# A two-layer hybrid decoder step on eight cores: first tiles on two rings, parameters and tiles for the second layer fetched earlier, squares in a buffer of their own

## The reference, cut to what matters

```
h = RMSNorm(x)
p = h @ w_in                      # 1024 -> 3456 columns
a_val, a_gate, a_z | b_h, b_b, b_c, b_z | c_u, c_v, c_z = split(p)
a   = a_val * sigmoid(a_gate)
y_a = silu(LayerNorm(conv31(a) + bias)) * silu(a_z)
y_b = b_b * conv3(b_c * b_h) * silu(b_z)
y_c = c_u * chunk_mix(LayerNorm(c_v)) * silu(c_z)   # causal 128x128 mix per head
x   = x + concat(y_a, y_b, y_c) @ w_out
```

## Time and profile before

| | us |
| --- | --- |
| median of 3 runs | 610.75 (609.86 to 610.85) |
| the profiled execution | 613.45 |
| span of its slowest core (core 1), first to last instruction | 611.6 |
| spans of cores 0 to 7 | 602.7, 611.6, 607.4, 599.5, 609.5, 598.7, 607.7, 599.1 |
| PE busy on core 1 | 582.4 (95% of the span) |
| DVE, ACT, POOL busy on core 1 | 453.0 (74%), 259.8 (42%), 94.7 (15%) |

### The profile page before, as it was taken

One profiled execution on the slowest core, in us unless ns is written; L12 is line 12 of the kernel. 1 busy time (PEld: TensorE's weight loads), 2 busy tenths in 40 slices (PEclk: granted clock), 3 DMA queues, 4 the chain that ended last, 5 costly groups with the idle time before them and its releaser, 6 DMA issues.

```text
span 611.6 us, 12509 instructions; the slowest of 8 cores (598.7 to 611.6 us)
## 1 busy us (share of the span) xinstructions
PE 582.4 (95%) x5002; PEld 330.3 (54%) x5002; DVE 453.0 (74%) x874; ACT 259.8 (42%) x467; POOL 94.7 (15%) x162
## 2 busy tenths in 40 slices
PE   7799998999999999899986999999999999999895
PEld 3545444466556656565642455545565665665552
DVE  2387955678886866587646967889987977876895
ACT  4345623234722732273327213732373274253463
POOL 3500501110110110011043020122011111200101
PEclk9899999999999999899998999999999999999999
DMA  8999997642683594789689989574146336607402
GB/s 180 180 152 222 168 190 128 178 74 70 111 203 52 122 145 142 174 183 229 136 152 214 184 123 250 148 144 156 48 125 141 126 108 154 167 31 108 105 1 103
DMA packets 71737, 86.00 MB, mean 141 GB/s; under 512 B 18944, under 2 KB 60096, under 8 KB 71680
## 3 DMA queue, kind: packets, MB, share of 16 engines
q1 hardware_dynamic: 48560, 60.78, 38.9%
q0 software_dynamic: 18752, 19.93, 24.8%
q10 hardware_dynamic: 4368, 4.51, 3.0%
HBM read 77.77 MB, written 29.81 MB: 176 GB/s over the span
## 4 chain that ended last, share of the span: by engine, by line
PE 83%; DMA 7%; DVE 5%; ACT 2%; issue 1%; SPq 1%; POOL 0%; DVEq 0%; POOLq 0%; ACTq 0%
PE pb L450 76%; PE pb L451 6%; DMA hst<-st_aT 3%; DMA w_in_sb<-w_in 3%; DMA xr<-x_scr 2%; PE pb L620 1%; DVE xr L418 1%; ACT tmp L409 1%; DVE xr L430 1%; SPq L440 1%; DVE xr L977 1%; DVE W L506 0%; DVE h_tm L430 0%; ACT L409 0%; ACT h_fm L409 0%
## 5 line engine op out<-in xcount | busy, mean ns | idle before, releaser
L450 PE MATMUL pb<-h_fm,w_in_sb 128*128 128x384 bf16 (+3 forms) x2032 | 371.6, 342 | 10.6 <-DVE a_t L430 4.6
L450 PEld LDWEIGHTS pb<-h_fm,w_in_sb 128*128 128x128 bf16 x2032 | 197.1, 99 | 170.4 <-issue 5.8
L409 ACT ACTIVATE tmp<-pb 128x384 f32<-128x384 f32 (+2 forms) x110 | 56.4, 518 | 146.7 <-PE pb L450 143.5
L450 PE MATMUL pb<-w_out_sb,mix 128*128 128x512 bf16 (+1 forms) x544 | 115.9, 379 | 0.0
L450 PEld LDWEIGHTS pb<-w_out_sb,mix 128*128 128x128 bf16 (+1 forms) x544 | 51.5, 98 | 61.6 <-issue 0.8
L409 ACT ACTIVATE tmp<-xr 128x1024 bf16<-128x1024 f32 (+2 forms) x52 | 53.8, 1035 | 66.5 <-DVE xr L418 41.6
L418 DVE TENSOR_TENSOR xr<-pb,xr 128x512 f32<-128x512 f32 (+1 forms) x72 | 47.6, 687 | 30.1 <-PE pb L450 29.9
L563 POOL TENSOR_SCALAR rstd<-ss 128x1 f32<-128x1 f32 (+1 forms) x46 | 14.8, 321 | 252.1 <-ACT tmp L409 251.8
L430 DVE SCALAR_TENSOR_TENSOR tmp<-z_ext,pc,tmp 128x384 f32<-128x384 bf16 (+1 forms) x60 | 37.7, 640 | 7.7 <-ACT tmp L409 7.1
L418 DVE TENSOR_TENSOR mix<-tmp 128x384 bf16<-128x384 f32 (+2 forms) x50 | 29.3, 590 | 14.6 <-ACT tmp L409 14.5
L430 DVE SCALAR_TENSOR_TENSOR h_tm<-xr,rstd,ng_b 128x1024 bf16<-128x1024 f32 (+1 forms) x30 | 37.7, 1277 | 1.9 <-POOL rstd L564 1.1
(11 more groups left out here) (108 smaller groups left out, 507.2 us busy)
## 6 DMA issues: line engine op xcount, KB each, us to landing
A<-a_scr SPq DMA_DIRECT2D x32, 309.0 KB, 7.9
w_in_sb<-w_in POOLq DMA_DIRECT2D x17, 512.0 KB, 23.2
xr<-x_in SPq DMA_DIRECT2D x16, 512.0 KB, 8.6
x_scr<-xr SPq DMA_DIRECT2D x16, 512.0 KB, 7.0
xr<-x_scr SPq DMA_DIRECT2D x16, 512.0 KB, 6.1
y_o<-xr SPq DMA_DIRECT2D x15, 512.0 KB, 3.1
w_out_sb<-w_out POOLq DMA_DIRECT2D x4, 1024.0 KB, 19.8
w_in_scr<-w_in POOLq DMA_DIRECT2D x7, 512.0 KB, 9.2
```

The costliest lines, as they stand in the source:

```text
L409: S.add("act", lambda e: e.activation(out=out, in_=in_, func=func, **kw), reads=reads, writes=writes, cost=170 + 0.833 * free_size(out) + ...
L450: return lambda e: e.matmul(out, lhsT, rhs, start=start, stop=stop)
```

## The change

The start: tile 1 goes on ACT's ring beside tile 0 on SP's, pieces 0 and 1 of `w_in` are issued at once, tiles 2 and 3 after tile 1 has landed, the other pieces after tile 0 was transposed. Each tile is turned and scaled by itself (`T_in`, in place of `T_half`). The identity matrix is made on POOL and no longer loaded; 28 matmuls on zeros instead of 30. ACT's squares write to a buffer of their own (`junk`) instead of one of the seven rotating `tmp` buffers.

Block 0 of layer 0: the saved rows (`hist_dma`) are loaded ahead of `w_out`, and `LN_out` moves into block 1. The layer boundary: the parameters of layer 1 are loaded in block 2 (`params_dma`, without the bias, which goes in two transfers instead of four at the end of layer 0); from the last layer-0 block on, the tiles of the block after next are loaded in `stage_B` of a block (no longer those of the next block at its begin); `w_out` of layer 1 is issued later; in layer 1 the stores of `h_scr` stand in front of the shifted loads of the convolution. `sa_h` is issued before `stage_B`. `stage_C` takes its fill-in work per half. At the tail the final norm of the last block but one is put behind `stage_stats` of the last block.

```diff
+        load_x(0, 0)
+        load_x(0, 1, (), "act")
+        xmark = [S.ops[-1].idx]
+        dma("sp", cst[:], consts, [], ["cst"])
 ...
-            load_win(0, i, xmark if i else ())
+            load_win(0, i)
+            if i == 1:
+                S.add("pool", lambda e: e.affine_select(out=ident_bf[:], in_=ones_bf[:], ...
+                break
 ...
+        for j in range(4):
+            hs = hslot()
+            H_norm(0, blocks[0].ids[j], 128, hs, False, ev if j > 1 else ())
+            T_in(j, hs)
+            if j == 0:
+                load_x(0, 2, xmark)
+                load_x(0, 3, xmark)
+                for i in range(2, len(PIECES)):
+                    load_win(0, i, mark())
+            if j == 1:
 ...
+                dummy(8)
+                A_half(0, 0)
+            if j == 2:
+                A_half(1, 0)
 ...
             if c == 0:
-                LN_out(l, blk, mark())
+                hist_dma(l, mark())
                 for hf in range(2):
                     load_wout(0, hf, mark())
 ...
+            if oi == 1:
+                LN_out(*prev, mark())
 ...
-            if not tail and oi > 1:
+            if not tail and 1 < oi < 5:
                 for t in nxt[1].ids:
                     load_x(nxt[0], t, mark())
 ...
-            a4_load(blk)
+            a4_store(blk)
+            if not dt:
+                a4_load(blk)
 ...
             if dt:
                 H_elem(oi + 1)
+                a4_load(blk)
                 H_turn(oi + 1)
 ...
-            stage_O(*prev)
+            fins = stage_O(*prev, tail)
 ...
+            if l == 0 and blk.i == 2:
+                params_dma(l + 1, mA)
 ...
+            if blk.i == 3:
+                dma("sp", sa_h[l], st_a[l, :, DSEQ:KA - 1, 0:WA], [], [("sah", l)], mC)
 ...
                 if c == 0 and tail:
                     stage_stats(l, blk)
+                    for f in fins:
+                        f(mark())
+                if c == 1 and 4 <= oi < len(order_b) - 2:
+                    for t in order_b[oi + 2][1].ids:
+                        load_x(1, t, mark())
 ...
             if final:
-                params_dma(l + 1, mark())
+                cbias_dma(l + 1, mark())
 ...
-            act(tmp[0:r, ti, 0:NMAX].bitcast(BF16), xr[0:r, s, :], AF.Square, XK(s), [tk, ("ss", k)],
+            act(junk[0:r, :], xr[0:r, s, :], AF.Square, XK(s), ["junk", ("ss", k)],
```

More of the change, by code:

```diff
@@ L464, in xrows, with load_x @@
             return (SEQ, NS) if t == SMP else (128 * t, 128)
[L466 removed]
+        def load_x(l, t, after=(), q="sp"):
             r0, r = xrows(t)
@@ L661, in HFM @@
         def HFM():
-            return hfm(0) + hfm(1) + [("hfj", cur["par"], j) for j in range(4)]
+            return hfm(0) + hfm(1) + [("hfj", cur["par"], j) for j in range(4)] + [("hf3", k) for k in range(8)]
         def proj_part(b, col, lo, hi, keys):
@@ L1077, in stage_O, with fin @@
                         rsq(rstd[0:r, k:k + 1], ss[0:r, k:k + 1], 1, [sk], [("rstd", k, "f")])
-                    for sl, xk in ([(slice(0, 512), [("x", s, 0)]), (slice(512, D), [("x", s, 1)])] if end
-                                   else [(slice(0, D), XK(s))]):
-                        stt(xr[0:r, s, sl], xr[0:r, s, sl], rstd[0:r, k:k + 1], fg_b[0:r, sl], ALU.mult, ALU.mult,
-                            xk + [("rstd", k, "f"), "fg"], xk)
-                        dma("sp", y_o[r0:r0 + r, sl], xr[0:r, s, sl], xk, [("y", t, sl.start)] + xk)
+                    def fin(after=(), s=s, r=r, k=k, t=t, r0=r0, end=end):
+                        for sl, xk in ([(slice(0, 512), [("x", s, 0)]), (slice(512, D), [("x", s, 1)])] if end
+                                       else [(slice(0, D), XK(s))]):
+                            stt(xr[0:r, s, sl], xr[0:r, s, sl], rstd[0:r, k:k + 1], fg_b[0:r, sl], ALU.mult, ALU.mult,
+                                xk + [("rstd", k, "f"), "fg"], xk, after=after)
+                            dma("sp", y_o[r0:r0 + r, sl], xr[0:r, s, sl], xk, [("y", t, sl.start)] + xk)
+                    if not late and not end:
+                        fin()
+                    else:
+                        fins.append(fin)
+            return fins
         def halo0(blk, after=()):
@@ L1102, in build_program @@
         wb = balloc()
-        for i in range(3):
-            pe([mm(pbank[wb][:, :], ones_bf[:], mix[:, 0, :], True, True) for _ in range(10)], ["ones", ("mix", 0)],
-               [pk(wb)], 10 * 300)
+        pe([mm(pbank[wb][:, :], ones_bf[:], mix[:, 0, :], True, True) for _ in range(28)], ["ones", ("mix", 0)],
+           [pk(wb)], 28 * 260)
         brel(wb)
@@ new lines, in build_program, with T_in @@
+            if i == 1:
+                S.add("pool", lambda e: e.affine_select(out=ident_bf[:], in_=ones_bf[:], pattern=[[1, 128]],
+                                                        compare_op=ALU.is_equal, fill=0.0, base=0,
+                                                        channel_multiplier=-1),
+                      reads=["ones"], writes=["ident_bf"], cost=400)
+                break
+        use(0, blocks[0])
+        def T_in(j, hs):
+            bs = [balloc(), balloc()]
+            V = [pbank[b][:].bitcast(BF16).rearrange("p (k t) -> p k t", k=8) for b in bs]
+            pe([(lambda e, k=k: e.transpose(V[k // 3 > 0][:, k, :], h_tm[:, hs, k * 128:(k + 1) * 128], ident_bf[:]))
+                for k in range(8)], [("htm", hs), "ident_bf"], [pk(b) for b in bs], 8 * 70)
+            wk = [[("hf3", k) if j == 3 else ("hfm", 0, k, j // 2)] for k in range(8)]
+            dst = h_fm[:, 0, 0:8 * NMAX].rearrange("p (k t) -> p k t", k=8)[:, :, 128 * j:128 * j + 128]
+            tt(dst[:, 3:8, :], V[1][:, 3:8, :], pc[:, 0, 3:8].unsqueeze(2).broadcast_to([128, 5, 128]), ALU.mult,
+               [pk(bs[1]), "pc"], sum(wk[3:8], []))
+            for k in range(3):
+                act(dst[:, k, :], V[0][:, k, :], AF.Copy, [pk(bs[0]), "pc"], wk[k], scale=pcol(0, k))
+            brel(*bs)
@@ L1130, in A_half @@
+        pre = [(balloc(), balloc()) for _ in range(2)]
         def A_half(c, hv):
             for b, col in zip(pre[c], (C_AV, C_AG)):
-                proj_part(b, col + 128 * c, 256 * hv, 256 * hv + 256, hfm(hv))
-        T_half(0)
-        ev = [max(o.idx for o in S.ops if o.eng == "act")]
-        m0 = mark()
-        H_norm(0, blocks[0].ids[2], 128, hslot(), False)
-        H_norm(0, blocks[0].ids[3], 128, hslot(), False, ev)
-        params_dma(0, m0)
-        S.add("pe", lambda e: [mm(pbank[pre[0][0]][:, :], ones_bf[:], mix[:, 0, :], True, True)(e) for _ in range(8)],
-              reads=["ones", ("mix", 0)], writes=[pk(pre[0][0])], cost=8 * 216, after=m0)
@@ L1150, in build_program, with dummy @@
-        A_half(1, 0)
+                proj_part(b, col + 128 * c, 256 * hv, 256 * hv + 256, hfm(hv) + [("hf3", k) for k in range(8) if hv])
+        def dummy(n):
+            S.add("pe", lambda e: [mm(pbank[pre[0][0]][:, :], ones_bf[:], mix[:, 0, :], True, True)(e) for _ in range(n)],
+                  reads=["ones", ("mix", 0)], writes=[pk(pre[0][0])], cost=n * 216, after=mark())
+        for j in range(4):
[8 more added lines that the diff above has]
+            if j == 1:
+                ev = [max(o.idx for o in S.ops if o.eng == "act")]
+                params_dma(0, mark())
+                cbias_dma(0, mark())
+                dummy(8)
+                A_half(0, 0)
+            if j == 2:
+                A_half(1, 0)
```

143 lines of the change are left out of this document (55 added, 88 removed).

## The result

| | before | after |
| --- | --- | --- |
| median of 4 runs each, us | 610.31 (607.88 to 610.85) | 618.18 (616.58 to 619.06) |
| ratio | | 1.0134, 95% interval 1.0098 to 1.0170: slower |
| PE, DVE, ACT, POOL busy on the slowest core, us | 582.4, 453.0, 259.8, 94.7 | 586.6, 454.3, 263.3, 99.1 |

The account below looks back on a forecast made before the run. PE was taken as the bound (83% of the chain), its pauses as winnable. Core 1: 0.3 + 1.7 + 4.9 + 1.6 + 6.1 - 3 + 0.4 = 12.0 us off 611.6; with 1.85 outside the span, less 1.35: 600.1 us, range 595 to 606.5.

Parts of the forecast that it names:

- squares into their own buffer: ACT's squares writing to `junk` instead of `tmp`: costed at nothing, since ACT is busy 42%.
- Rival D: Layer boundary: late tiles make ACT hold evacuations until PE's banks fill, clock falls; slower, 612.1 to 613 us; chance 0.13.
- My sign of being wrong: ACT waiting over 8 us at the squares, with PE waiting for ACT or DVE behind it.
- Layer boundary: Layer 0 to 1, core 1: gain 6.1 us from `a_t` wait and slow clock, loss 3 us at earlier squares.
- the 2 to 5 I named: Sign of being right: ACT waits 2 to 5 us for tiles, a stage earlier than before.
- Start: First projection begins earlier, but most is lost waiting for later `w_in` pieces; gain 0.3 us, bounds 0 and 2.5.
- Tail: Last block: moving final norms removes part of the `h_fm` wait; gain 0.4 us, bounds gain 1.2, loss 2.6.
- Saved rows: Block 0, layer 0: loading them before `w_out` removes the convolution's wait; gain 1.7 us on core 1, 5.2 on core 4.
- sums: End of layer 0: eight more projections in front cover PE's wait for `sums`; gain 1.6 us.
- wait without a releaser: Convolution of block 3: PE's instruction wait behind `sa_h` and `ng_b` goes, with slow clock; gain 4.9 us on core 1.

Follow-up runs that it names:

- the boundary alone: Kernel before, with layer-1 parameters loaded in block 2 and tiles of block 1 of layer 1 loaded early, squares still in `tmp`; 611.11 us, ratio 0.9965.
- held, start and tail as before: Changed kernel with all layer-1 squares held until the preceding block is finished, start transfers and final norms as before the change; 604.31 us, ratio 0.9858.

## Why the prediction was wrong, point by point

**The step that failed** is the sentence that costs "squares into their own buffer" at nothing because ACT is busy 42% of the time. The price of this edit is not ACT time but order. In `tmp` a square had to take its turn in seven rotating buffers, so the planner placed it behind the evacuations that stood before it in the code. In a buffer of its own nothing holds it but its tile, and the planner, whose cost for the load of a tile comes to 4.6 us where the first tile took 8.41 on core 3, moves it in front. This can be read from the order itself. ACT's list at the convolution of block 0 of layer 1, in the changed kernel and in a version that differs from it only by squares in `tmp` (only its order is known, no run was made of it):

```
changed kernel                              squares in tmp
ACTIVATE tmp<-pb 128x512 x3                 ACTIVATE tmp<-pb 128x512 x5
ACTIVATE junk,ss<-xr 128x1024 x3            ACTIVATE tmp<-pb,pc 128x256
ACTIVATE tmp<-pb 128x512 x2                 ACTIVATE tmp<-h_fm 128x512
ACTIVATE tmp<-pb,pc 128x256                 ACTIVATE tmp<-pb,pc 128x256 x2
ACTIVATE tmp<-h_fm 128x512                  ACTIVATE tmp<-h_fm 128x512 x2
ACTIVATE tmp<-pb,pc 128x256 x2              ACTIVATE tmp<-pb 128x448
ACTIVATE tmp<-h_fm 128x512 x2               ...
                                            ACTIVATE tmp,ss<-xr 128x1024
```

On the chip the same is seen from three sides: squares free and tiles early lose (changed kernel, 1.0094), squares held and tiles early win (0.9949 and, at both places, 0.9888), and in the boundary alone, squares in `tmp` and tiles early, ACT of core 3 does not wait at the boundary. That the buffer moves the squares is thus shown by the planner's order, and that their place costs the time by runs.

**I saw the mechanism and looked for it at one place only.** Rival D priced "ACT holds the evacuations until PE's banks are full, and the clock falls again" for the layer boundary. The diff loads tiles early in every later block as well; the second such place, one block on, has the same two edits and the worse transfers, and my sum has no term for it. It cost 6.9 us on core 1 and 7.0 on core 3. My sign of being wrong, a wait of ACT over 8 us, was set too high: it came on core 0 alone (9.47 us, in the middle), and the other cores lost 3.8 to 7.5 us there with waits of at most 6.8. Two figures of rival D don't add up either: without its term the sum is 597.1, so a standstill of 15.5 us and 1.5 us of clock make 614.1, not 612.1 to 613, and the median of 610.75 is reached at 12.2 us, not 13.5.

**Layer boundary.** The size was right on the core for which I worked it out. ACT stands on core 1 for 4.72 us in front of the first tile, inside the 2 to 5 I named, and for 1.30 and 0.38 in front of the next two; PE waits 0.53 + 1.45 + 0.40 us behind it:

```profile
300.29 1.06 ACT L409 ACTIVATE junk<-xr 128x1024 bf16<-128x1024 f32 x1 [4.72 <-DMA xr<-x_scr]
```

```profile
304.42 3.72 PE L450 MATMUL pb<-h_fm,w_in_sb 128*128 128x512 bf16 x16 [0.53 <-ACT tmp L409]
309.59 1.89 PE L450 MATMUL pb<-h_fm,w_in_sb 128*128 128x512 bf16 x8 [1.45 <-DVE h_fm L418]
```

Between the output projections of blocks 3 and 4 core 1 gains 8.1 - 3.4 = 4.7 us; predicted for this stretch were 6.1 - 3 + 1.6 = 4.7. That the two agree to a tenth is luck in part: set against the boundary alone (57.7 us on core 1, 61.3 in the changed kernel) the new place cost 3.6 us on core 1, and 3.0 to 6.9 over all cores (61.0 to 64.6 against 57.5 to 58.0).

**Start.** Gain 0.3 forecast, with 0 as the lower bound; it is a loss. The first output projection comes 1.1 us later on core 1, 2.3 on core 3, 1.3 in the mean of eight cores (107.5 to 108.8). I was right that the win is lost at the next piece, and wrong that this is the worst case. PE's start on core 3, two rows from before the change and then two from after it:

```profile
15.86 1.92 PE L450 MATMUL pb<-h_fm,w_in_sb 128*128 128x256 bf16 x16 [2.10 <-DMA w_in_sb<-w_in]
...
20.44 1.05 PE L450 MATMUL pb<-h_fm,w_in_sb 128*128 128x256 bf16 x8 [2.22 <-DMA w_in_sb<-w_in]
```

```profile
14.36 1.91 PE L450 MATMUL pb<-h_fm,w_in_sb 128*128 128x256 bf16 x16
20.80 1.89 PE L450 MATMUL pb<-h_fm,w_in_sb 128*128 128x256 bf16 x8 [4.54 <-DMA w_in_sb<-w_in]
```

Before, there were two waits with transposes in between, and the second projection took 1.05 us. Now the first is 1.5 us earlier, piece 1 lands at 20.76 us against 20.39, and the two waits have become one of 4.54 us, behind which the clock is at the lower level for the 7.0 us of the window above and the second projection takes 1.89 us. On core 3 tile 1, on ACT's ring, lands at 8.39 us, 8.81 before, and tile 0 beside it at 8.19, 4.98 before; piece 1 is issued 6.6 us earlier and lands no earlier. This agrees with what the Trainium skill says on the page DMA: Bandwidth & Descriptors, section Issuing engines are not separate DMA queues: transfers that ACT, SP or POOL start run on the same 16 DMA engines, and issuing them in parallel saves only the time of issuing. With the old transfers and the squares held the mean of the first output projection is 107.1 us, and 108.8 with the new; over all profiled versions with `T_in` it is 106.5 to 107.9 with the old (four) and 108.5 to 109.9 with the new (eight); the ratios of these two runs are 0.9852 and 0.9888, whose intervals overlap, but five of the six executions with the new transfers (606.06 to 608.30 us) are longer than the longest with the old (605.37).

**Tail.** A gain of 0.4 forecast, with a loss of up to 2.6 as the bound. The wait on `h_fm` left the last block of core 1 (core 3 had none), but the end is 1.9 us longer on core 3 (18.1 to 20.0 us from the last output projection on core 1, the same). DVE's tail there:

```profile
581.19 3.66 DVE L430 SCALAR_TENSOR_TENSOR xr<-xr,rstd,fg_b 128x1024 f32<-128x1024 f32 x3
...
595.82 1.68 DVE L418 TENSOR_TENSOR mix<-h_fm,szt 128x384 bf16<-128x384 f32 x3
599.17 3.93 DVE L418 TENSOR_TENSOR xr<-pb,xr 128x512 f32<-128x512 f32 x6 [1.68 <-PE pb L450]
```

The three moved norms take the 3.66 us I had counted as 3.84, `mix` is late, the groups of the last projection end late, and six additions stand in one row behind them. With the norms moved back most cores end the last block 1.2 to 2.1 us sooner (final norms early; held, start and tail as before): the move cost that much, inside my bound of 2.6. In the time of the slowest core it does not show; the intervals of these two runs are 1.6 and 2.3 us to either side.

**Saved rows, sums, wait without a releaser.** The wait for saved rows in layer 0, 0.67 to 3.59 us on seven cores before, is gone on every core; the 0.5 us that are left in its entry on core 1 stand at 440.03, in layer 1. For `sums` 0.40 us are left at the boundary of core 1, and the rest of its 1.8 us, 0.84 + 0.55, is new and lies in the middle; with all squares held no core waits for `sums`, so the eight projections in front do cover this wait. The pause without a releaser went on every core; that `sa_h` made it is not shown. From the first to the fourth output projection core 1 gained 4.5 us, of 1.7 + 4.9 = 6.6 forecast. In sum core 1 has -1.1 at the start, 4.5 up to block 3, 4.7 at the boundary, -6.9 in the middle, 1.0 in layer 1 and -1.9 at the end, 0.3 us in place of the 12.0 forecast.

**And the sum was made for the wrong cores.** Even with the loss in the middle taken out, the terms describe cores 1 and 4. Core 3 had 5.1 us of these waits where core 1 had 12.3, and won 0.5 + 0.5 us up to block 4, while what the middle and the end cost, they cost on every core. For the slowest of eight cores a gain counts only up to the next core, while a loss common to all counts in full.

## What to carry to other kernels

A buffer that is shared also orders: before an instruction gets a buffer of its own, look where a planner will then put it, and what stands behind it on its in-order engine at each place, not only where the change is aimed. An instruction that waits for a transfer belongs behind the work that empties PE's banks; a mark that holds it there turned 1.0094 into 0.9888 here with the same loads. In a program on several cores work out the sum for a core that has none of the waits, too.

## What the runs showed of the hardware

Not expected: issuing 2 MB of weights at 349 instead of 358 us cost some 1.3 to 1.7% in place of a gain (1.0261 against 1.0134 and 1.0094 of the changed kernel in its two measurements). At 349 us they meet the transposing reads on SP, whose issue then takes 14.04 us in place of 5.26 (core 3, `w_out` early and the changed kernel):

```profile
348.53 14.04 SPq L642 DMA_TRANSPOSE h_fm<-h_scr  x4
```

```profile
345.33 5.26 SPq L642 DMA_TRANSPOSE h_fm<-h_scr  x4
```

Before the change, with `w_out` issued at 345.13 us among them, the same four took 16.15 us. What SP issues behind them is late in turn: the tiles land 16.6 to 19.0 us later than in the changed kernel, 3.2 of them because this execution came later to the place. And PE at the start lost by beginning earlier: on core 3 one wait of 4.54 us had a granted clock of 0.51 beside and behind it for 7.0 us, where two waits of 2.10 and 2.22 us with work in between had left the next projection at full speed. On core 1 before the change a single wait of 2.34 us was followed by a first projection of 3.48 us at a granted clock of 0.52, where core 3 took 1.92 us behind 2.10; what makes the difference no run here shows.
